# Paged attention: two cache pages read into one tile, two neighbouring tokens to a partition

## The reference, cut to what matters

```python
def _gather_pages(pool, page_table):
    g = pool[page_table]
    return g.reshape((g.shape[0], g.shape[1] * g.shape[2]) + pool.shape[2:])
# in _fox:      cum = cumsum(concat(past log forget, new log forget))
# in _fox_attend:
s = einsum('bqhd,bkhd->bhqk', q_i, k) * ATTN_SCALE
s = s + cum_q - cum_k
s = where(k_idx <= pos, s, -inf)
out = einsum('bhqk,bkhd->bqhd', softmax(s), v)
```

## Time and profile before

| What | Value |
|---|---|
| Time, median of 3 runs | 3291.26 us (3290.3 to 3300.11) |
| Time of the profiled execution | 3285.07 us |
| Its span, first to last instruction | 3283.4 us |
| Mean granted TensorE clock | 0.843 of full speed |
| PE, DVE, ACT, POOL busy | 76%, 46%, 25%, 13% of the span |
| DMA over the span | 391.95 MB, mean 119 GB/s |
| First past attention (`fox`) | about 415 to 858 us |
| Past attention of `dilated` | about 2405 to 2706 us |

### The profile page before, as it was taken

One profiled execution on the slowest core, in us unless ns is written; L12 is line 12 of the kernel. 1 busy time (PEld: TensorE's weight loads), 2 busy tenths in 40 slices (PEclk: granted clock), 3 DMA queues, 4 the chain that ended last, 5 costly groups with the idle time before them and its releaser, 6 DMA issues. The chain is left out here.

```text
span 3283.4 us, 62739 instructions
## 1 busy us (share of the span) xinstructions
PE 2496.7 (76%) x24865; PEld 1925.4 (59%) x24865; DVE 1515.0 (46%) x2338; ACT 833.8 (25%) x1501; POOL 412.6 (13%) x606
## 2 busy tenths in 40 slices
PE   5858778878774777665499998597777777499996
PEld 1336466767453777634277776375456656277774
DVE  1032566776247444334545323425766653654223
ACT  0012444434122111002133211121643332233111
POOL 0010213333100000000211000102321110211000
PEclk9669778888786788757799999798988878799998
DMA  8932089998420000101033231130179981033221
GB/s 293 304 116 61 30 262 323 343 318 306 142 62 0 1 1 1 14 15 41 11 90 89 84 89 58 48 90 28 58 201 280 285 263 52 26 89 90 83 89 37
DMA packets 324210, 391.95 MB, mean 119 GB/s; under 512 B 26533, under 2 KB 225392, under 8 KB 323850
## 3 DMA queue, kind: packets, MB, share of 16 engines
q1 hardware_dynamic: 291690, 278.65, 27.5%
q0 software_dynamic: 32288, 110.12, 10.5%
HBM read 378.01 MB, written 10.70 MB: 118 GB/s over the span
## 5 line engine op out<-in xcount | busy, mean ns | idle before, releaser
L658 PE MATMUL bank<-yT,WH 128*128 128x288 f16 x3200 | 529.4, 289 | 117.7 <-DVE WL L695 117.7
L658 PEld LDWEIGHTS bank<-yT,WH 128*128 128x128 f16 x3200 | 315.3, 99 | 201.2 <-issue 91.0
L695 DVE SCALAR_TENSOR_TENSOR WL<-wring,WH 128x1024 f16<-128x1024 f32 x194 | 238.6, 1234 | 346.9 <-ACT WH L675 346.9
L1130 DVE TENSOR_TENSOR KL<-bank,KH 128x512 f16<-128x512 f32 x416 | 283.2, 688 | 210.4 <-ACT KH L1106 202.4
L1026 PE MATMUL bank<-cst,kslot 128*128 128x128 f32 x1664 | 313.1, 319 | 75.1 <-DMA kslot<-in_state_dil_k 43.5
L1106 ACT CAST KH<-bank 128x512 f16<-128x512 f32 x416 | 243.5, 586 | 403.3 <-PE bank L1026 403.2
L658 PE MATMUL bank<-uT,WH 128*128 128x288 f16 x2048 | 336.3, 287 | 11.0 <-DVE WL L695 11.0
L658 PE MATMUL bank<-yT,WL 128*128 128x288 f16 x1600 | 329.6, 288 | 0.0
L675 ACT ACTIVATE WH<-wring 128x1024 f16<-128x1024 f32 x194 | 203.4, 1053 | 293.6 <-PE bank L658 222.1
L1026 PEld LDWEIGHTS bank<-cst,kslot 128*128 128x128 f32 x1664 | 205.0, 159 | 105.2 <-DMA kslot<-in_state_dil_k 50.0
L658 PEld LDWEIGHTS bank<-uT,WH 128*128 128x128 f16 x2048 | 201.0, 98 | 62.9 <-issue 11.6
(11 more groups left out here) (380 smaller groups left out, 4082.7 us busy)
## 6 DMA issues: line engine op xcount, KB each, us to landing
kslot<-in_cache_fox_k SPq DMA_DIRECT2D x256, 256.0 KB, 5.8
vslot<-in_cache_fox_v POOLq DMA_DIRECT2D x256, 256.0 KB, 5.7
wring<-in_ada_w SPq DMA_DIRECT2D x96, 512.0 KB, 5.0
kslot<-in_state_dil_k SPq DMA_DIRECT2D x80, 512.0 KB, 10.4
vslot<-in_state_dil_v POOLq DMA_DIRECT2D x80, 512.0 KB, 14.6
wring<-in_mlp_up SPq DMA_DIRECT2D x64, 512.0 KB, 3.9
wring<-in_mlp_down SPq DMA_DIRECT2D x64, 512.0 KB, 3.9
wring<-in_ev_w_in SPq DMA_DIRECT2D x26, 512.0 KB, 3.8
```

The source lines that it names most:

```text
L658: last = nc.tensor.matmul(bank[b + h][:, 0:HALF], w[s % 2][:, c, :], x[:, s % parts * KC + c, h * HALF:(h + 1) * HALF], start=(s % parts = ...
L695: nc.vector.scalar_tensor_tensor(WL[s % 2][:, :, :], w[:, :, :], WSCALE, WH[s % 2][:, :, :], ALU.mult, ALU.subtract).then_inc(w_free, 1)
L1130: nc.vector.tensor_tensor(KL[i][:, :], turned[n % NT][:, :], KH[i][:, :], ALU.subtract).then_inc(lo_out, 1)
```

## The change

For `fox` two pages become one tile of 128 partitions x 1024 float32. The first page goes to partitions 0 to 63 and the second to partitions 64 to 127; a partition receives two neighbouring tokens of its page, which are 4 KB in one piece. Each page is still one DMA of 256 KB, now of 64 rows of 4 KB, and both DMAs of a tile count on one semaphore, for which the readers wait at 32. The left half of a tile holds the even tokens of both pages and the right half the odd ones; each half is one unit, so there are still 256 units. The key ring becomes 4 tiles and the value ring 8, as many bytes as before, and a slot is free when both of its units are used. POOL's maximum over partitions stays before the third tile of a sequence, which is now the fifth page. `decay` gets the layout to match: each `page_sums` is now eight smaller matmuls in place of two. `dilated` gets the new arguments with its old values, and nothing else.

```diff
@@ page_sums
                         pe.wait_ge(t_out, 4 * g + b + 1)
-                        o = bank[b][:, 0:256].rearrange("p (h g) -> p h g", h=8)
-                        nc.tensor.matmul(o, C["later"], lft[b][:, :, 0:PAGES], start=True, stop=False)
-                        nc.tensor.matmul(o, C["ones"], lft[b][:, :, PAGES:2 * PAGES], start=False, stop=True).then_inc(r_ok, 1)
+                        for a in range(2):
+                            o = bank[b][64 * a:64 * a + 64, 0:256].rearrange("p (h g e) -> p h g e", h=8, e=2)
+                            for e in range(2):
+                                nc.tensor.matmul(o[:, :, :, e], C["later"][:, e::2], lft[b][:, :, a:PAGES:2], start=True, stop=False)
+                                last = nc.tensor.matmul(o[:, :, :, e], C["ones"][:, 0:64], lft[b][:, :, PAGES + a:2 * PAGES:2], start=False, stop=True)
+                        last.then_inc(r_ok, 1)
@@ attend_past
-    def attend_past(nt, E, KR, VR, LEAD, chunk0, Q, KNEW, VNEW, load_k, load_v, bias_of, new_bias_of):
+    def attend_past(nt, E, TU, KR, VR, LEAD, chunk0, Q, KNEW, VNEW, load_k, load_v, bias_of, new_bias_of, LANDED=16):
-        nu = nt * E
+        nu = nt * TU
-            K = [sb(sc, f"kslot{i}", [P, 512 * E]) for i in range(KR)]
-            V = [sb(sc, f"vslot{i}", [P, 512 * E]) for i in range(VR)]
+            K = [sb(sc, f"kslot{i}", [P, 512 * TU]) for i in range(KR)]
+            V = [sb(sc, f"vslot{i}", [P, 512 * TU]) for i in range(VR)]
-                            sp.wait_ge(kt_ok, (t - KR + 1) * E)
+                            sp.wait_ge(kt_ok, (t - KR + 1) * TU)
-                            pool.wait_ge(v_used, ((t - VR + 1) * E + SG - 1) // SG)
+                            pool.wait_ge(v_used, ((t - VR + 1) * TU + SG - 1) // SG)
-                        t, e = divmod(n, E)
+                        t, part = divmod(n, TU)
-                        pe.wait_ge(k_in[t % KR], 16 * (t // KR + 1))
+                        pe.wait_ge(k_in[t % KR], LANDED * (t // KR + 1))
...
-                            pe.wait_ge(v_in[t % VR], 16 * (t // VR + 1))
+                            e = n % E
+                            pe.wait_ge(v_in[t % VR], LANDED * (t // VR + 1))
@@ fox
-                def load(sp, n, dst, done):
-                    page = sp.value_load(pt_sb[0:1, n:n + 1], min_val=0, max_val=319)
-                    sp.dma_start(dst[:, :], src[ds(page, 1), :, :].rearrange("a p n -> p (a n)")).then_inc(done, 16)
+                def load(eng, n, dst, done):
+                    for a in range(2):
+                        page = eng.value_load(pt_sb[0:1, 2 * n + a:2 * n + a + 1], min_val=0, max_val=319)
+                        eng.dma_start(dst[64 * a:64 * a + 64, :], src[ds(page, 1), :, :].rearrange("a (p e) n -> (a p) (e n)", e=2)).then_inc(done, 16)
...
-            attend_past(PAGES, 1, 8, 16, 2, 4, (QB, QH, QL), KNEW, VNEW, load_page("cache_fox_k"), load_page("cache_fox_v"), bias_of,
-                        lambda s: nbias[:, s, :, :])
+            attend_past(PAGES // 2, 1, 2, 4, 8, 2, 4, (QB, QH, QL), KNEW, VNEW, load_page("cache_fox_k"), load_page("cache_fox_v"), bias_of,
+                        lambda s: nbias[:, s, :, :], LANDED=32)
@@ dilated
-            attend_past(DILT, 2, 4, 8, 0, 0, (QB, QH, QL), KNEW, VNEW, load_tile("state_dil_k"), load_tile("state_dil_v"),
+            attend_past(DILT, 2, 2, 4, 8, 0, 0, (QB, QH, QL), KNEW, VNEW, load_tile("state_dil_k"), load_tile("state_dil_v"),
```

More of the change, by code:

```diff
@@ L1025, in turn @@
                         for j in range(4):
-                            last = nc.tensor.transpose(b[:, j * P:(j + 1) * P], K[t % KR][:, 512 * e + j * P:512 * e + (j + 1) * P], ident)
+                            last = nc.tensor.transpose(b[:, j * P:(j + 1) * P], K[t % KR][:, 512 * part + j * P:512 * part + (j + 1) * P], ident)
                         last.then_inc(kt_ok, 1)
@@ L1062, in values @@
                             n = s * nu + u
-                            t, e = divmod(n, E)
-                            pe.wait_ge(v_in[t % VR], 16 * (t // VR + 1))
+                            t, part = divmod(n, TU)
+                            e = n % E
+                            pe.wait_ge(v_in[t % VR], LANDED * (t // VR + 1))
                             for j in range(4):
                                 last = nc.tensor.matmul(o[32 * j:32 * j + 16, 256 * e:256 * e + P], st[:, u, 16 * j:16 * j + 16],
-                                                        V[t % VR][:, 512 * e + j * P:512 * e + (j + 1) * P], start=(u == 0), stop=False, skip_group_check=E > 1)
+                                                        V[t % VR][:, 512 * part + j * P:512 * part + (j + 1) * P], start=(u == 0), stop=False, skip_group_check=E > 1)
                         last.then_inc(v_used, 1)
```

## The result

The changed kernel takes 3421.72 us (median of 4 runs, 3411.07 to 3422.46) against 3290.78 us (3289.97 to 3300.11): 1.0384 times as long, 95% interval 1.0356 to 1.0411. The forecast was 3403, the likeliest case's own range 3369 to 3440. The profiled execution took 3411.07 us, with a span of 3409.4, which is 126.0 us over the span before.

What follows compares the result with a forecast made beforehand. It took the middle of the `fox` stage as bound by DMA about half the time, elsewhere by the key ring and TensorE. 3285.1 + 109 + 3 = 3397.1, with 6.2 for the median 3403 us; range 3283 to 3470.

Steps and rivals of the forecast that it cites:

- Which partitions one DMA writes: Middle part of the `fox` stage: half-partition DMAs fill the engines at 250 GB/s, 464 us against 355, +109 (0 to +193).
- dilated plateau: Profile before, dilated tiles 0 to 5: mean 258 GB/s at full DMA share, put down to partitions, not HBM gaps.
- rival A: `fox` stage: the halves share harder, 212 GB/s throughout, +193 +4 +3, 3491 us; chance 0.10.
- The first 50 us and the tail: Both ends of the `fox` stage: already under 243 GB/s (228 and 208), so they keep their length, 0.
- Count of instructions: DMA issues of SyncE and GpSimd: still 256 key and 256 value DMAs at unchanged cost, 0 (-18 to 0).
- Rows of 4 KB: Full windows of the middle part: longer rows might carry 5% more, at most 8 us; equal queue turns taken as 0.
- Rings in pairs: Key and value rings: waits for both pages only move, early value pages bring nothing, 0 (-11 to +25).
- rival C: `fox` stage: no sharing, low plateau from HBM gaps, rate over 370 GB/s; 3275 us, or 3291 without gain; chance 0.24.
- Page sums: adaLN stage: eight smaller matmuls per call take twice the work, +3 us (0 to +13).
- B: Middle part: the two queues write different halves and even out partly, 300 GB/s, +32 and +3, 3326 us; chance 0.12.

Runs made afterwards that it cites:

- e5: The changed kernel with page a on partitions a, a + 2, a + 4 and so on, bias layout not adapted: 3273.81 us against 3286.96 for the kernel before, ratio 0.9966.
- e2: The changed kernel with rows of 2 KB, each page still on 64 partitions, bias layout not adapted: 3454.28 us, ratio 1.0500 to the kernel before.
- e1: The changed kernel with only the placement undone: pages over all 128 partitions, rows of 2 KB, old page sums; 3280.87 us against 3291.07 for the kernel before.
- e4: The changed kernel with key pages of partitions 64 to 127 issued by ScalarE on its own queue: 3365.04 us, ratio 1.0224 to the kernel before.
- e7: The kernel before with dilated tiles 0 to 5 reading 128 rows two tokens apart, in one dimension of 128: 3240.73 us, ratio 0.9862.
- e8: The kernel before with the 16 groups of 8 rows in dilated tiles 0 to 5 lying 9 tokens apart instead of 16: 3290.28 us, ratio 1.0018.
- e3: The changed kernel with one 512 KB DMA per tile over all 128 partitions, 4 KB rows, neighbouring pages at fixed addresses: 3235.81 us, ratio 0.9833 to the kernel before.
- e12: The change with page a on every second partition and page sums to match: 3277.66 us against 3286.75 for the kernel before, ratio 0.9965.
- e10: The kernel before with the values of `fox` also issued by SyncE, merged with the keys in order of need: 3427.91 us, ratio 1.0437.

## Why the prediction was right

*Which partitions one DMA writes*: the step that decided, and right. I took 250 GB/s for the middle from the dilated plateau; it was 247. From the first key issue to the last the trace has +120.6 us against the +109 of the sum. Of the 12 more, 6 are 247 for 250 on the 116.1 MB, and about 4 are the 1.0 MB that the first 50 us didn't bring, worked off at 247. e5 shows the cause by itself, and e2 and e1 exclude the rivals. That the number came so close is in part luck. I tied the two streams by how the 16 engines share a DMA's rows (eight neighbouring partitions each), which no trace shows, and e5's finer form of that idea failed. The dilated plateau is slow for a reason in its 16 groups that stays open, and half-tile streams ran at 232 (e2), 247 and 277 GB/s (e4). e7 and e8 exclude the HBM gaps, which I had put aside by argument alone.

One reading under this term was wrong. I took the window of 212 GB/s in the earlier trace rows for the key queue alone and the one of 268 for both. The trace's queues (packets, MB, share; q0 GpSimd's, q1 SyncE's) say otherwise, first for 2460 to 2465 us, then for 2615 to 2620:

```profile
q0 software_dynamic: 146, 0.53, 50.7%
q1 hardware_dynamic: 145, 0.53, 50.5%
...
q1 hardware_dynamic: 289, 1.04, 79.0%
q0 software_dynamic: 90, 0.30, 23.0%
```

At 212 GB/s both queues move half, and at 268 the keys have most of it. So 212 was no price of a single queue, and what I wrote for and against rival A falls with it. The 258 is right: over the plateau the two queues have about half each.

*The first 50 us and the tail*: taken at 0, and too small. Counted from the first key issue, the first 50 us are these in the kernel before, in the changed kernel and in e5:

```profile
415.70:465.70 50.00, 38.84 (x604) 34.59 (x608) 34.23 (x57) 23.27 (x40) 3.23 (x6) 0.77 0.77 230
418.80:468.80 50.00, 33.85 (x497) 31.16 (x498) 26.99 (x43) 18.72 (x32) 2.17 (x4) 0.70 0.90 210
418.30:468.30 50.00, 35.78 (x554) 32.71 (x555) 29.03 (x47) 20.52 (x35) 2.26 (x4) 0.77 0.75 222
```

Before, SyncE's issue is the bound there: 43 pages in 50 us, one every 1.17, and 1.4 us of waiting for the ring. e5 has the change's longer issue (0.475 us) but full-width DMAs and falls to 222 GB/s. The change falls to 210, because there the half partitions bind too: from 425 to 445 us it has 224 GB/s at a share of 1.05.

The tail is 8.4 us longer, and 6.4 of them pass before GpSimd's last maximum. It comes 21.4 us after the last key issue instead of 15.0. In the kernel before, then in the changed one (start, us, operation):

```profile
818.52 0.52 POOL L1012 PARTITION_ALL_REDUCE amx<-cmx  x1 [7.89 <-DVE cmx L1159]
...
948.57 0.52 POOL L1015 PARTITION_ALL_REDUCE amx<-cmx  x1 [20.80 <-DVE cmx L1163]
```

That fits key pages that land 10.9 us after their issue at the median instead of 5.8, which no run tests by itself. From the maximum to the end it is 41.5 us for 39.5, and GpSimd's issue every 1.15 us still sets the pace there, as I had read it. The rings in pairs aren't the reason: e1's tail is as short as before (last key issue 803.0, last output 856.6 us).

*Count of instructions*: I took the cost of an issue as unchanged and looked only for a gain. GpSimd's fell by 0.03 us, SyncE's rose by 0.131. In the middle that costs nothing, since SyncE waits 188.3 us for the key ring between 465 and 930 us.

*Rows of 4 KB*: right in size where a DMA reaches both halves: the windows of 370 GB/s or more average 402 in e3 and 396 in e5, against 383. In the change the half partitions hide it. The page has 32288 packets on GpSimd's queue before and after, while SyncE's fall from 291690 to 275306, by 64 for each key page. So only the keys' packets changed, which fits what I read from the earlier trace rows.

*Rings in pairs*: 0 in the sum. With DMAs over all partitions e1 has -8 (-12 to -4), which is within the bounds and near rival C's -11 for the early value pages, though its waits don't show that they are the cause. Rival C was wrong on its condition.

*Page sums*: +3 taken, +7.6 measured (3 to 12), within 0 to 13. The work was mis-sized: I counted a call as 454 and 379 ns, but the trace has two records for each matmul, so the doubling adds 10.8 us of busy time and not 6.7. The 2.0 us that I counted as free cover little of it.

*The whole number*: the result is 18.7 us above the forecast. Of these, 14 are in the profiled execution: 12 up to the last key issue and 8 in the tail, less 6 behind the stage. The rest is the median, which lies 10.7 us above the profiled execution and not 6.2.

*Rivals*: A (212 GB/s throughout) was seen in no part as a whole, only in single windows such as 211 at 1.04 from 425 to 430 us. B asked for 300 GB/s; with two queues they evened out no further than single windows of up to 288. With three queues (e4) it reaches 277.

The page "SBUF — State Buffer" of the Trainium skill, "Door 1: The DMA port swizzle", gives the right sign: half of the partitions reach half of the ports. Its formula spreads every second partition over all ports, which agrees with e5. The 208 GB/s that I worked out from its 196 and the 6% of "Can I just issue two DMAs to hit both halves?" is an estimate, and the 247 of this stream is higher; the measurement decides.

## What to carry to other kernels

Read how many partitions one DMA reaches before you lengthen its rows: here half a tile cost a third of the full rate (383 to 247 GB/s), while rows of 4 KB for 2 KB brought 5%. When two small pieces must share a tile, lay them on every second partition (e12), not one above the other. Look for a stream in the same trace that already moves data as the change would. The rate taken from it, 250 GB/s, was 1% off here, but that the two streams are slow for one reason was never shown, so give such a number a wide range. Before you call a queue idle, read the queues of that window: a GpSimd that issues nothing can still have data on its way.

## What was not expected of the hardware

- A page whose number is read from a table costs SyncE 1.11 us an issue, so a stream of 256 KB pages from it alone ends at 236 GB/s (e10); the DMA instruction itself is 0.34 of it. GpSimd's takes 1.15.
- The same 64 rows of 4 KB cost SyncE 0.469 us to issue, against 0.338 for 128 rows of 2 KB and 0.599 for e2's 64 partitions with two rows each.
- At a full share, half-tile streams moved more the more queues wrote: 224 GB/s with nearly the keys alone (425 to 445 us), 231 with the values alone (one window of 5 us in the tail), 247 with two queues, 277 with three (e4). No run separates the number of queues from which halves are in flight together.
